# Three attention stages: GpSimd divides the probabilities by their row sums, and the transposes run three steps behind the scores

## The reference

```python
# fox: 16 heads of 64, causal, per block of 128 queries
s = jnp.einsum('bhqd,bhkd->bhqk', qi, kt)
s = s + fqi[..., None] - fk[:, :, None, :]
s = jnp.where(kpos[None, :] <= qpos[:, None], s, -jnp.inf)
p = jax.nn.softmax(s, axis=-1)
return jnp.einsum('bhqk,bhkd->bhqd', p, vt)
...
o = o * jax.nn.silu(z.astype(jnp.float32))
# win and mla: 8 heads each; win has 3 neighbouring blocks and 256 context keys and a sink
# logit in the softmax, mla has all 1024 + 256 keys
s = jnp.einsum('bqhgd,bkhd->bhgqk', q, k).astype(jnp.float32) * scale
p = jax.nn.softmax(s, axis=-1)
return jnp.einsum('bhgqk,bkhd->bqhgd', p.astype(v.dtype), v)
```

## Time and profile before

| | us |
|---|---|
| median of 3 runs (4484.34 to 4494.48) | 4492.06 |
| span of the profiled execution, first to last instruction | 4462.5 |
| fox stage, 64 steps | 249.3 |
| win stage, 40 steps | 145.6 |
| mla stage, 32 steps | 278.7 |

### The profile page before, as it was taken

The page is one execution under the profiler, slowest core; times in us unless marked ns, Lnnn a source line. Parts: engine busy times, 40 slices in busy tenths (PEclk is TensorE's granted clock), DMA queues, the critical chain, the costliest instruction groups (busy, mean ns, idle before and its releaser), DMA issues. The chain is left out here.

```text
span 4462.5 us, 74337 instructions
## 1 busy us (share of the span) xinstructions
PE 4110.1 (92%) x30096; PEld 2628.8 (59%) x30096; DVE 2364.5 (53%) x4884; ACT 1132.6 (25%) x2569; POOL 230.0 (5%) x281
## 2 busy tenths in 40 slices
PE   7996899999899999996999999989989995999997
PEld 4443756888667788674555445558757773333332
DVE  6408334433676554746555555534435556666664
ACT  2011222212575323832200001021135632000001
POOL 0100000000121000000000000000000000000000
PEclk9998999999999999997999999999999997999998
DMA  7658221132421112116567767740161114888986
GB/s 292 242 89 344 76 76 39 67 107 94 164 91 67 74 61 97 33 58 267 226 248 272 281 256 279 269 155 21 60 209 43 21 59 166 323 341 326 344 332 224
DMA packets 133594, 757.41 MB, mean 170 GB/s; under 512 B 14336, under 2 KB 52992, under 8 KB 97904
## 3 DMA queue, kind: packets, MB, share of 16 engines
q1 hardware_dynamic: 108048, 670.05, 40.1%
q0 software_dynamic: 20272, 64.76, 5.3%
q10 hardware_dynamic: 5040, 19.37, 1.2%
HBM read 663.46 MB, written 91.19 MB: 169 GB/s over the span
## 5 line engine op out<-in xcount | busy, mean ns | idle before, releaser
L440 PE MATMUL psum<-w_ring,arena 128*128 128x256 f32 (+1 forms) x2784 | 610.7, 378 | 19.8 <-PEq L199 8.5
L440 PEld LDWEIGHTS psum<-w_ring,arena 128*128 128x128 f32 x2784 | 522.8, 192 | 91.1 <-issue 21.2
L3362 PE MATMUL psum<-arena 128*64 128x512 f32 x2048 | 452.5, 593 | 2.6
L3392 PE MATMUL psum<-arena 128*128 128x512 f32 x1024 | 447.9, 595 | 3.7 <-DVE arena L3659 0.9
L440 PE MATMUL psum<-arena,w_ring 128*128 128x256 f32 x1600 | 352.9, 380 | 6.4 <-DVE arena L495 3.5
L3362 PE MATMUL psum<-w_ring,arena 128*64 128x512 f32 x1536 | 343.8, 597 | 2.8 <-issue 2.8
L3392 PEld LDWEIGHTS psum<-arena 128*128 128x128 f32 x1024 | 191.9, 190 | 237.6 <-issue 231.2
L440 PEld LDWEIGHTS psum<-arena,w_ring 128*128 128x128 f32 x1600 | 301.8, 190 | 49.5 <-DVE w_ring L536 3.6
L3362 PEld LDWEIGHTS psum<-arena 128*64 128x64 f32 x2048 | 150.8, 137 | 273.1 <-issue 271.0
L3510 ACT ACTIVATE arena<-psum 128x512 f32<-128x512 f32 x128 | 76.6, 598 | 911.6 <-PE psum L3362 911.6
L1851 PE MATMUL psum<-arena 48*128 48x512 f32 (+5 forms) x1440 | 292.1, 516 | 8.9 <-PEq L1464 3.5
(11 more groups left out here) (429 smaller groups left out, 5376.9 us busy)
## 6 DMA issues: line engine op xcount, KB each, us to landing
w_ring<-in_wstream SPq DMA_DIRECT2D x162, 2048.0 KB, 10.3
arena<-in_wstream SPq DMA_DIRECT2D x97, 2048.0 KB, 7.8
x_rows<-arena SPq DMA_DIRECT2D x26, 512.0 KB, 2.7
w_ring<-in_wstream ACTq DMA_DIRECT2D x6, 2048.0 KB, 7.8
arena<-x_rows SPq DMA_DIRECT2D x18, 512.0 KB, 7.3
xn_rows<-arena POOLq DMA_DIRECT2D x18, 512.0 KB, 7.3
arena<-f_rows SPq DMA_DIRECT2D x8, 1024.0 KB, 7.6
arena<-x_rows SPq DMA_DIRECT2D x8, 1024.0 KB, 9.1
```

What stands on the lines that cost most here:

```text
L440: last = self.cr.nc.tensor.matmul(out, l, r, start=(start and k == 0), stop=(k == len(pairs) - 1), skip_group_check=True)
L3362: last = nc.tensor.matmul(cr.bank[bank][HT * h:HT * (h + 1), :], left[:, k], right[:, 4 * h + k, :], start=(start and k == 0), stop=(k == ...
L3392: last = nc.tensor.matmul(cr.bank[YB[h]][:, :], hid[:, k], W[4 + h][:, k, :], start=(k == 4), stop=(k == 3))
```

## The change

Instead of dividing the output, the kernel divides the probabilities while the queries are still in the partitions. POOL does it in place in `s_buf`, one `TENSOR_SCALAR` for each head over the whole width of a step (`scale`), when DVE has written the inverse row sums. The transposes wait for POOL (`sd`) and no longer for ACT's exponential (`pr`). `spread`, the `COPY` into `rinv`, ACT's copy to `r_buf` and the multiplication by it are gone. In fox DVE now multiplies the output straight from PSUM by the gate z, and POOL no longer does; in win and mla DVE copies the output. To give POOL time, transposes, copies and values run three steps behind the scores instead of two, with four slots instead of three. DVE takes the output of two steps out of PSUM at odd iterations, after the reciprocal.

```diff
@@ SP @@
-                        sp.wait_ge(gated, (last_of[p - 2] + 1) // 2)
+                        sp.wait_ge(ev, (last_of[p - 2] + 1) // 2)
@@ POOL @@
+            def scale(s):
+
+                pool.wait_ge(inv, s + 1)
+                for h in range(2):
+                    v = s_buf[s % 4][:, h, 0:steps[s].width]
+                    nc.gpsimd.tensor_scalar(v, v, rsum[:, s % 4, h:h + 1], None, ALU.mult).then_inc(sd, 1)
+
-                    if s >= 3 and s % 2 == 0:
-                        e = (s - 3) // 2
-                        pool.wait_ge(ev, e + 1)
-                        o, z = gate(2 * e)
-                        nc.gpsimd.tensor_tensor(o, o, z, ALU.mult).then_inc(gated, 1)
-                pool.wait_ge(gated, NS // 2)
+            for s in range(NS + 2):
+                if s < NS and own is not None:
+                    own_mask(s)
+                if s >= 2:
+                    scale(s - 2)
+            pool.wait_ge(sd, 2 * NS)
@@ PE @@
-                        pe.wait_ge(pr, 2 * s + h + 1)
+                        pe.wait_ge(sd, 2 * s + h + 1)
...
-            def spread(s):
-
-                pe.wait_ge(inv, s + 1)
-                for h in range(2):
-                    last = nc.tensor.matmul(o_bank(s)[h * HD:(h + 1) * HD, 2 * P + s % 2 * P:2 * P + (s % 2 + 1) * P], rinv[:, s % 3, h], cr.const(C_ID),
-                                            start=True, stop=True, skip_group_check=True)
-                last.then_inc(pv, 1)
...
-                ng = len(steps[s - 2].groups) if 2 <= s < NS + 2 else 0
+                ng = len(steps[s - 3].groups) if s >= 3 else 0
...
-                if s >= 3:
-                    spread(s - 3)
                 for g in range(ng):
-                    values(goff[s - 2] + g)
+                    values(goff[s - 3] + g)
@@ ACT @@
-                if s >= 4 and s % 2 == 0:
-                    e = (s - 4) // 2
-                    act.wait_ge(pv, 2 * e + 2)
-                    if e >= 2:
-                        act.wait_ge(ev, e - 1)
-                    copy(r_buf[:, e % 2], cr.bank[6 + e % 2][:, 2 * P:4 * P]).then_inc(rc, 1)
@@ DVE @@
-                if s >= 4 and s % 2 == 0:
-                    e = (s - 4) // 2
-                    dve.wait_ge(rc, e + 1)
-                    nc.vector.tensor_tensor(steps[2 * e].o, cr.bank[6 + e % 2][:, 0:2 * P], r_buf[:, e % 2], ALU.mult).then_inc(ev, 1)
                 if 1 <= s <= NS:
                     v = s - 1
                     dve.wait_ge(pr, 2 * v + 2)
-                    if v >= 3:
-                        dve.wait_ge(pv, v - 2)
...
-                    ln(nc.vector.reciprocal(rsum[:, v % 3], rsum[:, v % 3]))
-                    nc.vector.tensor_copy(rinv[:, v % 3], rsum[:, v % 3].unsqueeze(2).broadcast_to([P, 2, HD])).then_inc(inv, 1)
+                    nc.vector.reciprocal(rsum[:, v % 4], rsum[:, v % 4]).then_inc(inv, 1)
+                if s >= 5 and s % 2:
+                    e = (s - 5) // 2
+                    dve.wait_ge(pv, 2 * e + 2)
+                    o = cr.bank[6 + e % 2][:, 0:2 * P]
+                    if gate is not None:
+                        nc.vector.tensor_tensor(steps[2 * e].o, o, gate(2 * e), ALU.mult).then_inc(ev, 1)
+                    else:
+                        nc.vector.tensor_copy(steps[2 * e].o, o).then_inc(ev, 1)
```

98 lines of the change are left out of this document (49 added, 49 removed).

## The result

The changed kernel takes 4562.65 us (median of 5 runs, 4561.03 to 4566.35), the kernel before on the same chip 4492.06: ratio 1.0162, 95% interval 1.0149 to 1.0174. It is 71 us slower where 26 us faster was forecast.

What follows compares the result with a forecast made beforehand. It took PE's list to bound mla and a chain from engine to engine to bound fox and win. Fox -13, win -10 and mla -3 made -26 us: 4492 to 4466, range 4440 to 4495.

Steps and rivals of the forecast that it cites:

- A one-input operation must lie between; I take 1.2 ns a column: POOL's scaling: price between a memset's 0.8 and a two-input TENSOR_TENSOR's 2.1 ns a column, so POOL stays in time.
- rival 3: POOL becomes the bound in fox's wide steps, missing from about 1.7 ns; +12 us at 2.5 ns; chance 0.17 with mild form.
- The COPY on the path, -16.2: Fox's four wide steps: removing DVE's COPY behind the reciprocal saves 2.0 us a pair of heads, 16.2 us for 8.
- The distance: One more step at each stage's end has transposes without scores beside them: fox +2, win +1, mla +1.8 us.
- No slower: Fox: with 1024-wide transposes beside 128 columns of scores instead of 512, PE's group-to-group chain gets no slower, nor faster.
- Rival 2: Given back: fox's wide transposes beside narrow scores cost what the COPY saved; together -7 us, 4485; chance 0.17.
- The products, -5.1 and -6.4: Without spreading products, values begin 0.16 us sooner a step: mla -5.1, win -6.4, fox -5.1 us.
- DVE beside POOL: DVE's remaining operations, such as `maxima`, are not slowed by a busy POOL: nothing; 13 us in fox if each lost 0.1.
- edge term of +1.8: End of mla: one more step without scores beside its transposes leaves PE idle 0.91 and 0.89 us, +1.8 us.

Runs made afterwards that it cites:

- eight columns: Changed kernel, but POOL scales only the first 8 columns of each head, the rest of the scaling left out; 4467.02 us, ratio 0.9987 to the kernel before.
- half the columns: Changed kernel, but POOL scales only the left half of each head's columns; ratio 0.9993 to the kernel before.
- the run with two inputs: Changed kernel, own order of blocks, with the scaling as TENSOR_TENSOR with the inverse sum broadcast instead of TENSOR_SCALAR; ratio 0.9998 to the kernel before.
- the run with the cut: Changed kernel with TENSOR_TENSOR scaling, old block order, scaling split at 512-column groups so PE's first group waits for the first part alone; ratio 0.9993.
- new order: Fox's query blocks as 0,1,6,7,2,3,4,5 instead of 0,1,4,5,6,7,2,3; on the changed kernel scaling only 8 columns a head: 4448.25 us, ratio 0.9947.

## Why the prediction was wrong

The stages against the kernel before, from one profile each:

| us | forecast | eight columns | scaling's price (changed less eight columns) | changed kernel |
|---|---|---|---|---|
| fox | -13 | +1.8 | +52.7 | +54.5 |
| win | -10 | -9.4 | +20.8 | +11.4 |
| mla | -3 | -0.3 | +3.3 | +3.0 |
| sum | -26 | -7.9 | +76.8 | +68.9 |

- *The step that failed first* is "A one-input operation must lie between; I take 1.2 ns a column". It is 2.5, above both of its bounds, and worth 71 of the 95 us between forecast and result (changed kernel less half the columns, whose 1.25 ns is nearly the assumed price). Another 5 us are what the scaling costs at the assumed price, which the forecast put at nothing; the last 18 are the structure, below. The bounds came from a memset and from another operation; neither bounds a TENSOR_SCALAR. The 8-column row could give the fixed part alone. The prediction had written 2.5 down in rival 3 with the right place and a threshold, and dismissed it with the same sentence on inputs ("one input less than the row that gives 2.1").
- *Rival 3* had mechanism and onset (1.7 ns) right and was too small at 2.5 ns: "fox -13 + 30" became +54.5, "win -2" became +11.4. It counted the miss of the wide steps as 3.8 us a pair; it is 6.5 (37.4 - 30.9). Even its sum for 2.85 ns, +35, is half of the loss measured at 2.5.
- *The COPY on the path, -16.2*: mis-sized. Alone it is worth 3.3 us in fox, at three steps 9.6. "DVE's list is nearly without gaps" was read off busy time, but DVE's next scores come from PE's chain, and the time went into the wait for them.
- *The distance*: "In fox I take +2" failed. By itself it costs 22 us there, and the order of blocks gave 15.5 of such a loss back. "No slower" was argued for one chain, not for the step around it. Rival 2 names this, and with a free scaling the kernel is 6.9 us faster than before, the -7 of rival 2, though only fox comes out stage by stage (its +2 against +1.8; win -5 against -9.4, mla -3 against -0.3). Its sign, fox no shorter with DVE 26 us less busy, came too.
- *The products, -5.1 and -6.4*: held where PE is full. In mla the mean middle step is 8.17 us in every kernel without them and 8.40 before, 0.22 shorter for a forecast 0.16. Win's 136.2 for a forecast 135 is in part luck, since the terms miss and cancel: the products and what went with them gave 8.9 and the COPY 2.7, where 6.4 and nothing were forecast, and the distance cost 2.2 where it was to give 3.4. In fox they and what went with them are worth 10.7.
- *DVE beside POOL*, "I put this at nothing": held. `maxima` of 512 columns still takes 0.69 us on average beside a POOL that is busy 263 of 304 us, and no wait of DVE for a mask appears.
- *mla*: -3.6 (275.1) in two runs with PEclk 0.99 there, and up to +2.4 in others at 0.96. The last values of the stage, with no scores ahead of them, take 2.35 us in the kernel before, 3.53 in the run with two inputs and 4.53 in the changed kernel. So the edge term of +1.8 is right in its waits and leaves out that PE comes out of them at the lower clock. The difference among the runs lies at the two ends of the stage: from the 6th to the 27th step all kernels without the products take 171.6 us, and the rest behind it takes 54.7 us in the run with two inputs and 59.8 in the run with the cut, with PEclk at 0.96 and 0.79 in the last 40 us. Why the clock there differs among kernels that have the same list is open.
- *The clock in fox*: not foreseen; some 6 us of the 53 could be won back from it, in fox's profile and not resolved in the total.

Also open: how much of fox's 235.6 us a complete kernel could reach. The new order needs the wide scalings sooner than POOL can give them even at 1.67 ns; a mask moved behind the scaling was not tried.

## What to carry to other kernels

Don't bound the price of an operation by others that seem simpler or harder on the same engine: put the instruction itself, at its width, into a kernel before a whole list rests on it, and try its sibling forms, since one form of the same multiplication was a third cheaper and decided between 1.6% slower and level. An engine that is handed a job inside a pipeline of fixed distance has one step's time for its widest step, not the average over steps; where it just misses, let the consumer wait for the first part alone. And when a distance is lengthened, write down what now stands beside what: here a change of the blocks' order was worth more (15 us) than the COPY that was removed, and its sign turned with the price of the scaling. And where a sum of terms comes out, as win's did, check the terms one by one before trusting them.

## What the runs showed of the hardware

- GpSimd on 128 partitions: TENSOR_SCALAR 2.5 ns a column and 0.28 us with a scalar from memory, 0.21 with an immediate; TENSOR_TENSOR with a broadcast second operand 1.67 ns and 0.19 us.
- DVE's TENSOR_SCALAR on the same data: 0.53 ns a column and 0.21 us when alone (883 ns for 1280), a mean of 528 ns for 128 columns beside POOL's masks. POOL's 1280 columns took 4.21 us beside it instead of 3.51.
- TensorE's granted clock fell to 0.66 to 0.71 in 5 us windows where PE waited for POOL again and again; 896 products more in fox's waits brought the stage from 0.88 to 0.98 and made it 5.8 us shorter.
